# A one-element tile moved ahead of the weight buffers, which then start 64 bytes higher in each partition

## The reference, cut to what matters

```
proj = xm @ w_in_even                       # 2048 x 7184, tokens of x and of the context
y @ w_out_even; xm @ w_in_odd; y @ w_out_odd
n @ w_in; q @ w_uq; kv @ w_ukv; o @ w_attn_o; y @ w_rnn_o; mix @ w_out
q = x @ w_peer_q                            # which of 16384 experts a token takes
act = gelu(einsum('tkd,td->tk', peer_u[e], xc))   # done here as a dense product with all of peer_u
out = einsum('tkd,tk->td', peer_v[e], gc * act)   # and with all of peer_v
gate = sigmoid(rms_norm(h) @ w_ple_gate); h + gate * (p @ w_ple_proj)
```

## Time and profile before

| | |
|---|---|
| executions | 3709.67, 3711.86, 3721.02 us |
| profiled execution | 3727.31 us, span 3724.7 us |
| TensorE matmul busy | 97% of the span |
| VectorE, ScalarE, GpSimd busy | 56%, 42%, 52% |
| DMA | 716.33 MB, 192 GB/s over the span |
| mean granted TensorE clock | 0.986 |

### The profile page before, as it was taken

How to read it: one execution, slowest core, us unless ns; L and a number is a source line. 1 busy time by engine, 2 the same in 40 slices (tenths; PEclk the granted TensorE clock), 3 DMA queues, 4 the chain that set the end, 5 groups by cost and what they waited for, 6 DMA issues and landing times.

```text
span 3724.7 us, 71312 instructions
## 1 busy us (share of the span) xinstructions
PE 3602.5 (97%) x29880; PEld 3478.3 (93%) x29880; DVE 2102.4 (56%) x3057; ACT 1564.1 (42%) x1986; POOL 1954.6 (52%) x788
## 2 busy tenths in 40 slices
PE   6999998999998999999999999999999999999998
PEld 3799897979998989999999999999999999999998
DVE  6686466883635566463124787873444666534345
ACT  5412433333344444464444444334444444444453
POOL 0137682008174849718988840028887000388876
PEclk9999999999999999999999999999999999999999
DMA  8557661855553535455555555445555555555543
GB/s 331 196 193 259 264 245 61 324 216 202 226 215 130 182 113 211 163 182 191 188 178 190 189 184 203 171 171 185 187 183 180 182 186 184 181 185 187 183 166 126
DMA packets 98405, 716.33 MB, mean 192 GB/s; under 512 B 11040, under 2 KB 11168, under 8 KB 12064
## 3 DMA queue, kind: packets, MB, share of 16 engines
q1 hardware_dynamic: 97056, 703.65, 51.9%
q10 hardware_dynamic: 1152, 9.87, 0.7%
HBM read 711.38 MB, written 2.10 MB: 192 GB/s over the span
## 4 chain that ended last, share of the span: by engine, by line
PE 82%; DVE 10%; DMA 2%; POOL 2%; ACT 2%; issue 2%; DVEq 0%; SPq 0%; POOLq 0%; ACTq 0%
PE bank L544 52%; PE bank L1091 19%; DMA ring<-in_w 2%; POOL unit_lo L481 2%; PE bank L596 2%; PE bank L702 2%; DVE unit_lo L1828 1%; PE bank L573 1%; DVE ada_acc L1629 1%; PE bank L1042 1%; ACT unit_hi L1138 1%; DVE unit_lo L1712 1%; PE bank L516 1%; PE bank L641 1%; PE bank L811 0%
## 5 line engine op out<-in xcount | busy, mean ns | idle before, releaser
L481 POOL TENSOR_TENSOR unit_lo<-ring,unit_hi 128x1024 fp32r<-128x1024 f32 x778 | 1939.0, 2507 | 1706.3 <-ACT unit_hi L1138 1705.2
L1138 ACT ACTIVATE unit_hi<-ring 128x1024 fp32r<-128x1024 f32 x1204 | 1239.4, 1056 | 1194.7 <-PE bank L544 439.6
L544 PE MATMUL bank<-xl_hi,unit_hi 128*128 128x256 f32 x4688 | 1317.4, 281 | 16.9 <-POOL unit_lo L481 5.5
L544 PE MATMUL bank<-xl_lo,unit_hi 128*128 128x256 f32 x4688 | 1304.1, 278 | 0.0
L544 PE MATMUL bank<-xl_hi,unit_lo 128*128 128x256 f32 x4688 | 1304.0, 278 | 0.0
L544 PEld LDWEIGHTS bank<-xl_hi,unit_hi 128*128 128x128 f32 x4688 | 886.0, 189 | 23.9 <-issue 9.7
L544 PEld LDWEIGHTS bank<-xl_hi,unit_lo 128*128 128x128 f32 x4688 | 886.2, 189 | 0.0
L544 PEld LDWEIGHTS bank<-xl_lo,unit_hi 128*128 128x128 f32 x4688 | 884.3, 189 | 0.5
L1091 PE MATMUL bank<-w_r,unit_hi 128*128 128x256 f32 x4096 | 723.9, 281 | 4.1 <-DVE w_r L2677 4.1
L1091 PEld LDWEIGHTS bank<-w_r,unit_hi 128*128 128x128 f32 x4096 | 628.4, 190 | 4.4 <-issue 4.4
L1091 PE MATMUL bank<-w_r,unit_lo 128*128 128x256 f32 x2048 | 575.5, 281 | 0.0
(11 more groups left out here) (459 smaller groups left out, 5055.0 us busy)
## 6 DMA issues: line engine op xcount, KB each, us to landing
ring<-in_w SPq DMA_DIRECT2D x669, 1024.0 KB, 4.8
resid<-in_xT ACTq DMA_DIRECT2D x1, 2048.0 KB, 15.6
tmp_ctx<-in_ctxT ACTq DMA_DIRECT2D x1, 2048.0 KB, 11.5
sgu_rows<-in_sgr ACTq DMA_DIRECT2D x1, 2048.0 KB, 8.9
rnn_gates<-in_rgw ACTq DMA_DIRECT2D x1, 2048.0 KB, 9.0
out<-resid SPq DMA_DIRECT2D x4, 512.0 KB, 2.6
con<-in_con ACTq DMA_DIRECT2D x1, 512.0 KB, 3.3
con<-in_con ACTq DMA_DIRECT2D x1, 448.0 KB, 7.8
```

Of the source, the lines that this page charges most:

```text
L481: pool.tensor_tensor(lb[b][:], ring[slot][:, f * HALF:(f + 1) * HALF], hb[b][:].bitcast(F32), ALU.subtract).then_inc(lo_done, 1)
L544: mm = pe.matmul(bank[(s.t0 + tile[m]) % TILES][:, 0:T], w[b][:, (i % 8) * P:(i % 8 + 1) * P], mv[x][:, k, :], start=(k == 0 and w is hb a ...
L1138: act.activation(hb[b][:], ring[slot][:, f * HALF:(f + 1) * HALF], ACT.Copy).then_inc(hi_done, 1)
```

## The change

`tick` is taken from behind `rstd` and placed first. It takes 64 bytes of each partition there as before, so everything from `ring0` to `rstd` starts 64 bytes higher: `ring`, `unit_hi`, `unit_lo` and `resid` now start at 64 above a multiple of 128. `lam_s`, `z0` and all tiles of `zone` stay.

```
@@ -203,6 +203,7 @@
+        tick = fixed("tick", [1, 1], F32)
         ring = [fixed(f"ring{i}", [P, UNIT], F32) for i in range(RING)]
         hb = [fixed(f"unit_hi{i}", [P, HALF], F32R) for i in range(NBUF)]
         lb = [fixed(f"unit_lo{i}", [P, HALF], F32R) for i in range(NBUF)]
@@ -215,7 +216,6 @@
         erow = fixed("erow", [64, T], F32)
         acol = fixed("acol", [P, 2, 4, 4], F32)
         rstd = fixed("rstd", [P, T], F32)
-        tick = fixed("tick", [1, 1], F32)
         lam_s = fixed("lam_s", [P, KC], F32)
```

## The result

The changed kernel took 3809.76 us (median of four executions, 3806.31 to 3817.51) against 3716.44 us for the kernel before (four, 3709.67 to 3721.90): a ratio of 1.0255, with a 95% interval of 1.0229 to 1.0281. The forecast was 3712 us with a range up to 3742. Of the executions of the kernel before that ran beside `lo_up_128` and `zone_up_160`, one was in a slow state and took 14,591 us; no median or range here counts it.

A forecast was written before the change was run, and what follows sets the result against it. The prediction took TensorE's matmuls, mainly those of lines 544 and 1091, to bound the kernel. Every term was put at 0 us, so the forecast stayed at the median of before, 3711.9 us, with a range of 3658 to 3742 us.

The forecast's parts named there:

- What bounds the kernel: TensorE, busy 3602.5 of 3724.7 us; 71% of the chain that ended last is the matmuls of lines 544 and 1091.
- Instructions, VectorE, ScalarE, loads: No instruction added, removed or moved; new tile places cost VectorE, ScalarE and the 1 MB loads nothing: 0 us each.
- Matmuls, one operand at a time: Lines 544 and 596: whether one float32r operand starts at a multiple of 128 bytes costs nothing, 0 us.
- Matmuls, both operands together: All float32r matmuls: placing both operands alike, which the trace of before can't show, was taken as 0 us.
- The bounds: Long stretches of float32r matmuls, at 4.4 ns each: 48 us that could go, 47 us that could be lost.
- rival "slower": Fast matmuls turn slow: peer_u0 and peer_u1, 27 us, 3739 us, chance 0.15; all fast stretches, 3759 us, chance 0.09.
- A third distance: Sign in the profile after: matmul starts neither 113.3 nor 117.8 ns apart would show placement acting in a new way.
- case "faster": All slow stretches become fast because equal placement avoids a collision: 3664 us, or 3657 with the short ones; chance 0.12.
- The two read ports: TensorE reads moving operand and weights through separate ports and never waits on anyone; by that rule the sum is 0.

The follow-up runs named there:

- lo_up_128: The kernel before with acol placed between unit_hi and unit_lo, so unit_lo and resid move up 128 bytes: 3681.36 us, ratio 0.9915.
- zone_up_160: The kernel before with the zone of the activations raised by 160 bytes: 3835.64 us, ratio 1.0328.
- hi_lo_up_64: The kernel before with tick placed between ring and unit_hi, so unit_hi, unit_lo and resid move up 64 bytes and ring stays: 3813.89 us.
- both_up_64: The changed kernel with the zone of the activations raised by 64 bytes as well: 3715.78 us.
- zone_up_64: The kernel before with only the zone of the activations raised by 64 bytes: 3840.26 us.
- fixed_up_256: The kernel before with cond and acol placed first, so ring, unit_hi, unit_lo and resid move up 256 bytes: 3701.38 us, ratio 0.999.
- zone_up_128: The kernel before with the zone of the activations raised by 128 bytes: 3766.71 us, ratio 1.0156.
- fixed_up_128: The kernel before with acol placed first, so ring, unit_hi, unit_lo and resid move up 128 bytes and the zone stays: 3768.79 us.
- w_r_up_64: The kernel before with only the two w_r tiles that move in line 1091 raised by 64 bytes: 3737.48 us, ratio 1.0062.
- zone_up_32: The kernel before with the zone of the activations raised by 32 bytes: 3800.19 us, ratio 1.025.

## Why the prediction was wrong, point by point

**What bounds the kernel.** Right. The 91 us lie in the matmuls of lines 544 and 1091, and reach the end almost undiminished.

**Instructions, VectorE, ScalarE, loads.** Right, each 0: 1056 and 1221 ns, 4.8 us, and in hi_lo_up_64 `ring`'s place had no share that shows. The estimate from the Trainium skill (DMA: Bandwidth & Descriptors, How a descriptor splits into AXI transactions), 0.6 us for starts further above a multiple of 256, is too small for any run here to show or to deny.

**Matmuls, one operand at a time.** Right: in both_up_64 the weights start 64 above a multiple of 128 and the moving operand at a multiple, and both levels are as before. The sign that was named for an error here, that lines 596 and 907 change alone, did not come: they went from 229.0 and 228.9 to 232.4 and 232.3 ns, together with all other float32r matmuls.

**Matmuls, both operands together.** This is the step that failed: the term that was put at 0 us measured 89 (80 in line 544, 9 in line 1091). The prediction named it as the one thing that the trace couldn't show, and gave it 0 because "no address that did vary had any effect". All those addresses varied by multiples of 512 bytes. The period is 256, so each of them left the distance modulo 256 where it was: the trace had 25,776 matmuls of lines 544 and 1091 and a single distance, and the argument drew on a variation that could not have shown anything. The second argument, that stage `xr` changes its rhythm with everything in place, is true and proves less than it was made to: both levels exist at one distance, and the distance sets which levels there are.

**The bounds.** They were too narrow for the same reason. The loss was bounded by the nearest rows, fast matmuls that turn slow at 4.4 ns, 47 us. But 117.8 ns was the slow level of one distance, not the slowest there is: at 0 and 96 the level is 120.0, 6.7 ns above the fast one. The rival "slower" had the right sign and mechanism, with a chance of 0.24 for both its forms, and the size of neither. "A third distance" was named as the sign that the placement acts in a way that the trace of before doesn't have, and that is what the trace after shows.

The ends were also hung on the wrong time. The slow and fast matmuls were counted in the profiled execution of 3727 us, and their cost was taken off and added to the median of 3712. The kernel without a slow level, lo_up_128, took 3681 us and not the 3664 or 3657 of the case "faster"; those with nearly all matmuls slow took 3767 and 3769, not 3759. This is 10 to 20 us and doesn't decide the miss.

**The two read ports.** The Trainium skill (SBUF — State Buffer, Who interferes with whom) has TensorE's two read ports independent and TensorE waiting on no one. The measurement decides against taking this as "placement costs nothing": moving two tiles by 64 bytes took line 1091 from 117.8 or 113.3 ns to 120.0. No run here tests whether another engine can slow TensorE.

**What is shown and what isn't.** Shown: the pace of a float32r matmul depends on the distance between its two operands' addresses modulo 256, and on neither address alone, in lines 544 and 1091 (both_up_64, zone_up_64, fixed_up_256, zone_up_128 beside fixed_up_128, w_r_up_64). Argued only: that two reads collide in the memory, the loading of the next weights and the moving operand. The experiments by place in the group of three didn't confirm it. Open: what sends a stage to 113.3 or 117.8 at distance 192, and why the slow level is gone in lo_up_128.

## What to carry to other kernels

Where matmuls follow each other without a gap, compute their distance from start to start, stage by stage; if equal matmuls show two distances, try the tiles at other offsets from each other, in steps of 64 bytes over 256, and look at both pairs and mixtures. Take the map from the shape that you run: the one above is for 256 columns, and another shape puts the same distances in another order (below). Write the distances between tiles into the allocation on purpose, since a harmless-looking edit of the list of tiles can cost 2.5%. And before saying that an address has no effect, ask by which steps it varied: only variation that is not a multiple of the period can speak.

## What the runs showed of the hardware that was not expected

Start-to-start distances of a 128x128 float32r matmul with 256 columns were mostly 113.3, 117.8, 118.3, 118.7 or 120.0 ns by the distance of the operands modulo 256, at a granted clock of 0.99 to 1.00 in the windows compared. At a distance of 192 a whole stage of 3072 matmuls took either 348.4 or 362.1 us, in one execution of the same program. With the weights' rests another 128 bytes up, six executions took 3679 to 3687 us, where the kernel before spreads over 3689 to 3734.

The record holds one thing more. In lines 573, 596 and 907 the roles are exchanged: the activations are the weights, and 512 columns of `unit_hi` or `unit_lo` move. Their distance is 64 in the kernel before, 128 in the changed one, 0 in zone_up_64 and 32 in zone_up_32; the longest piece of line 596 in each of the four, in this order (start us, us, what):

```profile
787.15 60.70 PE bank L596 x264
...
797.96 61.63 PE bank L596 x264
...
801.00 60.13 PE bank L596 x264
...
799.40 61.87 PE bank L596 x264
```

From start to start these are 229.0, 232.4, 227.2 and 233.3 ns. So a distance of 0, the worst for 256 columns, is the best of the four here. Matmuls of plain float32 show nothing of it: those of line 641 stand 215.8 ns apart in all four kernels.
